# Eight consecutive rows per partition in the expert up weights of a two-block transformer kernel

## The chip, the cores and the metric

The kernel runs on one core of a Trainium2 chip. The metric is the device time of one execution in microseconds. Weights and scratch tensors lie in HBM; the core's 16 DMA engines bring them into SBUF, which has 128 partitions.

## The reference, cut to what matters

Two transformer blocks run in a row on 1024 tokens of width 1024, all in float32, with a context of 256 tokens beside them. The first block has two layers, each ending in a mixture of experts in which each of 16 experts picks its 128 tokens (and, in the first layer, 32 context tokens); the second block has one layer with 32 experts of which each token picks two. What the change touches is the path from a normed row into the experts:

```python
h = rmsnorm(xl, norm2_g) * (1 + sc2) + sh2
aff = jax.nn.softmax((h @ router_w).astype(jnp.float32), axis=-1)
top_aff, idx = lax.top_k(jnp.swapaxes(aff, 1, 2), cap)
xg = jax.vmap(lambda hb, ib: hb[ib])(h, idx)
hid = jax.nn.silu(jnp.einsum('becd,edf->becf', xg, w_gate)) * jnp.einsum('becd,edf->becf', xg, w_up)
y = jnp.einsum('becf,efd->becd', hid, w_down) * top_aff[..., None].astype(h.dtype)
```

`sc2` and `sh2` are the second modulation vectors. They and `norm2_g` have one number for each of the 1024 features. The contraction over the feature `d` (1024) is cut into 8 chunks of 128. Any split of the 1024 features into 8 groups of 128 gives the same sums, as long as the rows `h`, the router's weights, the expert weights and the modulation columns use the same one. The second block is alike, with gate and up weights side by side in one tensor `w_expert_up_2` of 1024 x 1024 per expert.

## The kernel before, in words

The program is a list of stages, each with its own buffers and semaphores and a barrier at its end. Within a stage each engine has its instruction list written out by hand: SP and ACT issue direct DMAs, POOL (GpSimd) issues gathers and scatters with indices, PE multiplies and transposes, DVE (VectorE) and ACT (ScalarE) do the rest. `X` holds the token rows in SBUF, 128 tokens to a tile. `KD` is 8, the number of feature chunks. A tensor read as `(k p)` puts feature `128 k + p` into chunk `k`, partition `p`.

- `Modulating` (from L103) computes the modulation columns of a layer. `load_small` (L132) brings the two gains and four bias vectors as 48 rows of 128 into `small` by six DMAs; `turn_small` (L146) transposes them on PE, `take_small` (L150) copies the result to `smallT`. `products` multiplies with 4 MB of weights per group, `turn` (L174) transposes the two result rows in 8 pieces of 128, `take` copies them, and `finish` (L193) combines them on POOL into `cols`. Groups 0 to 2 are the first modulation, 3 to 5 the second. It runs beside the stages `setup`, `l0out`, `l0route` and `l1route`.
- `route_choice` (L1615), the stages `l0route` and `l1route`: SP loads the router weights `rw` (L1667), then the small vectors and the modulation weights. For each tile ACT writes the normed row `xn` (L1694, three buffers) and issues its store to the scratch tensor `XN`; PE transposes it in 8 pieces (L1749); DVE and ACT apply the columns of half the chunks each. Scores, softmax and the choice of the tokens by DVE follow. A buffer of `xn` is free once its store has landed.
- `choice_experts` (L1918), the stages `l0exp` and `l1exp`: for each expert SP issues the loads of `wg` (L1958), `wu` (L1959) and `wd` (L1962), 2 MB each, two experts deep; `wg` and `wu` wait until the expert two before has been multiplied, `wd` until its down product is done. POOL gathers the 128 (and 32) chosen rows from `XN` (L1970), two experts ahead, and scatters the results into `F` (L1984). PE turns the gathered rows (L2009), DVE applies the columns into `xT` (L2070), PE multiplies with `wg` and `wu` (L2026) and with `wd` (L2043).
- `mix_dispatch` (L3047), the stage `disp`: the same norm, store, transpose and scoring for the second block (L3306, L3347, L3355), and the first loads of the block experts.
- `block_experts` (L3384), the stage `bexp`: blocks of 128 rows, each with the weights of its expert, in a loop over pairs of blocks.

## Time and profile before

| what | value |
|---|---|
| runs of the kernel | 4721.94, 4724.09, 4727.69 us (median 4724.09) |
| span of the profiled execution | 4732.4 us |
| PE busy | 4229.9 us, 89% |
| DVE, ACT, POOL busy | 2033.2, 1069.4, 738.1 us |
| bytes moved by DMA | 769.59 MB, mean 163 GB/s |

The span runs from the first to the last record of one profiled execution; it lies 8.3 us above the median of the unprofiled runs. Busy times are sums of instruction durations. The stages in question lie at 997 to 1094 us (`l0route`), 1095 to 1570 (`l0exp`), 2400 to 2493 (`l1route`), 2493 to 2870 (`l1exp`), the dispatch up to 3982 and `bexp` from there to 4700. In `l0exp` and `l1exp` there are 96 loads of 2 MB, 64 of them of gate and up weights.

### The profile page before, as it was taken

To read this page: it belongs to the slowest core of one execution; us is meant where nothing else is said; L and a number is where in the kernel's file an instruction comes from. 1 tells how busy PE (TensorE), PEld (TensorE's weight loads), DVE (VectorE), ACT (ScalarE), POOL (GpSimd) and SP (SyncE) were. 2 spreads that over 40 slices of the span, in tenths; PEclk is the share of its full clock that TensorE was granted. 3 is DMA by queue.
4 is the path that set the end of the run, shared out by engine and by line. 5 is a ranking of instruction groups with operands and counts; after the bars stand their busy time and mean duration, and the time that the engine had idled before them with its cause. 6 is when DMAs were issued, how large, how long until landed. Compare 5 with 4: busy or idle time off the path is not lost. (4 is left out here: it accounts for less than half of the span.)

```text
span 4732.4 us, 59744 instructions
## 1 busy us (share of the span) xinstructions
PE 4229.9 (89%) x22975; PEld 2790.0 (59%) x22975; DVE 2033.2 (43%) x3879; ACT 1069.4 (23%) x2077; POOL 738.1 (16%) x851
## 2 busy tenths in 40 slices
PE   6998999977999798999968997999788896999996
PEld 4664556445888565566436885776566454444443
DVE  1223556135555322556254452111686666333332
ACT  1112346030000110335130001110564421111111
POOL 0110000301111011000301100000550330222221
PEclk8998999988999899999978998999899897999998
DMA  7115110367887411401169995111532115999997
GB/s 252 36 47 125 23 42 7 129 254 273 274 267 252 138 62 57 108 1 48 44 250 326 338 327 168 49 37 42 144 86 87 59 40 209 316 334 339 334 334 244
DMA packets 366851, 769.59 MB, mean 163 GB/s; under 512 B 59716, under 2 KB 136172, under 8 KB 365384
## 3 DMA queue, kind: packets, MB, share of 16 engines
q1 hardware_dynamic: 337032, 653.92, 40.2%
q0 software_dynamic: 23856, 90.19, 7.4%
q10 hardware_dynamic: 5712, 22.02, 1.2%
q8 instruction: 172, 2.82, 0.2%
q14 instruction: 79, 0.65, 0.0%
HBM read 650.62 MB, written 115.45 MB: 162 GB/s over the span
## 5 line engine op out<-in xcount | busy, mean ns | idle before, releaser
L3537 PE MATMUL bexp_gu<-X,bexp_xT 128*128 128x512 f32 x512 | 227.6, 598 | 3.0 <-DVE bexp_xT L3557 3.0
L3537 PE MATMUL bexp_gu<-bexp_wu,bexp_xT 128*128 128x512 f32 x512 | 225.1, 592 | 3.1 <-DVE bexp_xT L3557 3.1
L625 PE MATMUL p_ring<-p_hT,p_wc 128*128 128x256 f32 x1008 | 220.4, 381 | 4.8 <-DMA p_wc<-in_w_in 4.8
L625 PEld LDWEIGHTS p_ring<-p_hT,p_wc 128*128 128x128 f32 x1008 | 192.3, 191 | 31.6 <-issue 5.2
L3564 DVE TENSOR_SCALAR bexp_ex<-bexp_ex 128x512 f32<-128x512 f32 x32 | 15.1, 471 | 368.7 <-ACT bexp_ex L3492 368.7
L633 PE MATMUL p_ring<-p_wt,p_hT 128*128 128x400 f32 (+2 forms) x480 | 170.8, 516 | 0.0
L3537 PEld LDWEIGHTS bexp_gu<-X,bexp_xT 128*128 128x128 f32 x512 | 97.0, 192 | 119.8 <-issue 116.5
L3537 PEld LDWEIGHTS bexp_gu<-bexp_wu,bexp_xT 128*128 128x128 f32 x512 | 95.9, 190 | 117.7 <-issue 117.7
L1117 PE MATMUL l0mla_scores<-l0mla_kT,l0mla_qT 96*128 96x512 f32 (+1 forms) x312 | 142.9, 546 | 21.1 <-DMA l0mla_qT<-RT 15.3
L2026 PE MATMUL l0exp_gu<-l0exp_xT,l0exp_wg 128*128 128x160 f32 x1024 | 155.0, 305 | 4.5 <-DVE l0exp_xT L2070 4.5
L2026 PE MATMUL l0exp_gu<-l0exp_xT,l0exp_wu 128*128 128x160 f32 x1024 | 151.1, 301 | 1.5 <-DMA l0exp_wu<-in_exp_w_up 1.5
L2026 PEld LDWEIGHTS l0exp_gu<-l0exp_xT,l0exp_wg 128*128 128x128 f32 x1024 | 143.7, 192 | 11.4 <-issue 6.2
L3451 POOL TENSOR_TENSOR bexp_y<-bexp_y,bexp_og 128x1024 f32<-128x1024 f32 x32 | 75.0, 2344 | 481.6 <-ACT bexp_y L3486 481.6
L2043 PE MATMUL l0exp_acc<-l0exp_wd,l0exp_hid 128*32 128x256 f32 (+1 forms) x768 | 144.1, 455 | 2.6 <-DVE l0exp_hid L2085 2.6
L2026 PEld LDWEIGHTS l0exp_gu<-l0exp_xT,l0exp_wu 128*128 128x128 f32 x1024 | 144.0, 192 | 1.9 <-DMA l0exp_wu<-in_exp_w_up 1.9
L1117 PE MATMUL l1mla_scores<-l1mla_kT,l1mla_qT 96*128 96x512 f32 (+1 forms) x288 | 133.8, 551 | 12.3 <-DMA l1mla_qT<-RT 12.3
L3486 ACT ACTIVATE bexp_y<-bexp_acc,slot_gates 128x512 f32<-128x512 f32 x64 | 44.0, 687 | 419.6 <-PE bexp_acc L3525 419.6
L633 PEld LDWEIGHTS p_ring<-p_wt,p_hT 128*128 128x128 f32 x480 | 91.1, 190 | 76.1 <-issue 38.3
L2026 PE MATMUL l1exp_gu<-l1exp_xT,l1exp_wg 128*128 128x128 f32 x1024 | 127.4, 279 | 3.0 <-DMA l1exp_wg<-in_exp_w_gate 3.0
L2026 PEld LDWEIGHTS l1exp_gu<-l1exp_xT,l1exp_wg 128*128 128x128 f32 x1024 | 123.2, 195 | 10.6 <-issue 7.2
L2026 PE MATMUL l1exp_gu<-l1exp_xT,l1exp_wu 128*128 128x128 f32 x1024 | 125.7, 276 | 3.0 <-DMA l1exp_wu<-in_exp_w_up 3.0
L633 PE MATMUL l0proj_ring<-l0proj_wt,l0proj_hT 128*128 128x464 f32 x320 | 126.2, 552 | 0.0
(683 smaller groups left out, 8392.9 us busy)
## 6 DMA issues: line engine op xcount, KB each, us to landing
X<-in_w_expert_up SPq DMA_DIRECT2D x32, 2048.0 KB, 16.0
bexp_wu<-in_w_expert_up SPq DMA_DIRECT2D x32, 2048.0 KB, 16.7
l0exp_wg<-in_exp_w_gate SPq DMA_DIRECT2D x16, 2048.0 KB, 9.3
l0exp_wu<-in_exp_w_up SPq DMA_DIRECT2D x16, 2048.0 KB
l0exp_wd<-in_exp_w_down SPq DMA_DIRECT2D x16, 2048.0 KB, 12.6
l1exp_wg<-in_exp_w_gate SPq DMA_DIRECT2D x16, 2048.0 KB, 9.5
l1exp_wu<-in_exp_w_up SPq DMA_DIRECT2D x16, 2048.0 KB
l1exp_wd<-in_exp_w_down SPq DMA_DIRECT2D x16, 2048.0 KB, 13.1
```

Source lines behind the costliest of these rows:

```text
L625: mm = nc.tensor.matmul(out[:, i * PC:(i + 1) * PC], wc[:, k, b * 128:(b + 1) * 128], hT[ch % 2][:, k, :], start=(k == 0), stop=(k == KD - 1))
L633: mm = nc.tensor.matmul(out[:, at_out:at_out + n], hT[ch % 2][:, k, t * 128:(t + 1) * 128], wt[:, k, s:s + n], start=(k == 0), stop=(k == ...
L1117: mm = nc.tensor.matmul(scores[u % NBUF][:, at:at + n], qT[p % 2][a][:, row:row + 128], k[:, r:r + n], start=True, stop=True)
L2026: mm = nc.tensor.matmul(gu[g % 2][:, h, :], w[j][:, k, f * 128:(f + 1) * 128], xT[j][:, k, :], start=(k == 0), stop=(k == KD - 1))
L2043: mm = nc.tensor.matmul(acc[g % 3][cap * q:cap * (q + 1), 0:n_y], hid[j][:, f, at[s]:at[s] + cap], wd[j][:, f, at_y:at_y + n_y], start=(f ...
L3451: nc.gpsimd.tensor_tensor(y[j][:, :], y[j][:, :], og[:, :], ALU.mult).then_inc(weighed[j], 1)
L3486: nc.scalar.activation(y[j][:, c * 512:(c + 1) * 512], acc[c][:, :], ACT.Copy, scale=gates[:, bass.ds(i * B + j, 1)]).then_inc(y_ready[j], 1)
L3537: mm = nc.tensor.matmul(gu[h][:, :], xT[j][:, k, :], wu[j][h][:, k, :], start=(k == 0), stop=(k == KD - 1))
L3564: nc.vector.tensor_scalar(ex[:, :], ex[:, :], 1.0, None, ALU.add).then_inc(steps[j], 1)
```

## The change

The split of the features changes from `(k p)` to `(p k)`: chunk `k`, partition `p` now holds feature `8 p + k`, so that partition `p` needs the eight consecutive rows `8 p` to `8 p + 7` of a weight matrix. All that meets in the contraction follows: router weights, gate and up weights, the normed rows (ACT reads `X` with a step of eight elements and writes `xn` in the new order, so `XN` holds permuted rows), and the second modulation columns. The three small vectors of the second modulation are no longer transposed but loaded directly into `smallT` with eight numbers per partition; the transposes of the rows in groups 3 and 4 take every eighth element. The down weights and the first modulation stay as they are.

```diff
     def load_small(self, eng):
-        parts = [self.gain1, self.gain2] + [self.b[g * D:(g + 1) * D] for g in (0, 1, 3, 4)]
-        for i, src in enumerate(parts):
+        for i, src in enumerate([self.gain1] + [self.b[g * D:(g + 1) * D] for g in (0, 1)]):
             eng.dma_start(self.small[i * KD:(i + 1) * KD, :], src.rearrange("(k p) -> k p", p=128)).then_inc(self.small_in, 16)
+        for i, src in enumerate([self.gain2] + [self.b[g * D:(g + 1) * D] for g in (3, 4)]):
+            eng.dma_start(self.smallT[:, 3 + i, :], src.rearrange("(p k) -> p k", k=KD)).then_inc(self.small_in, 16)
...
-        self.nc.tensor.transpose(self.turned[:, 0:48], self.small[:, :], self.identity[0:48, 0:48]).then_inc(self.small_turned, 1)
+        self.nc.tensor.transpose(self.turned[:, 0:24], self.small[:, :], self.identity[0:24, 0:24]).then_inc(self.small_turned, 1)
...
         for k in range(KD):
-            tp = self.nc.tensor.transpose(self.turned[:, 64 + 2 * k:66 + 2 * k], self.rows[n % 2][:, k * 128:(k + 1) * 128], self.identity[0:2, 0:2])
+            chunk = slice(k * 128, (k + 1) * 128) if self.groups[n] < 3 else slice(k, D, KD)
+            tp = self.nc.tensor.transpose(self.turned[:, 64 + 2 * k:66 + 2 * k], self.rows[n % 2][:, chunk], self.identity[0:2, 0:2])
...
-                sp.dma_start(rw[:, :, 0:E], router_w.rearrange("(k p) e -> p k e", p=128)).then_inc(w_in, 16)
+                sp.dma_start(rw[:, :, 0:E], router_w.rearrange("(p k) e -> p k e", k=KD)).then_inc(w_in, 16)
...
-                    nc.scalar.activation(xn[n % 3][:, :], X[:, t, :], ACT.Copy, scale=ssum[:, t:t + 1]).then_inc(normed, 1)
+                    nc.scalar.activation(xn[n % 3][:, :].rearrange("p (k a) -> p k a", k=KD), X[:, t, :].rearrange("p (a k) -> p k a", k=KD), ACT.Copy,
+                                         scale=ssum[:, t:t + 1]).then_inc(normed, 1)
...
-                    sp.dma_start(wg[j][:, :, :], w_gate[e].rearrange("(k p) n -> p k n", p=128)).then_inc(gate_in[j], 16)
-                    sp.dma_start(wu[j][:, :, :], w_up[e].rearrange("(k p) n -> p k n", p=128)).then_inc(up_in[j], 16)
+                    sp.dma_start(wg[j][:, :, :], w_gate[e].rearrange("(p k) n -> p k n", k=KD)).then_inc(gate_in[j], 16)
+                    sp.dma_start(wu[j][:, :, :], w_up[e].rearrange("(p k) n -> p k n", k=KD)).then_inc(up_in[j], 16)
...
-                            sp.dma_start(wu[j][h][:, :, :], w_up[bass.ds(e, 1), :, h * FF:(h + 1) * FF].rearrange("e (k p) n -> p (e k) n", p=128)).then_inc(landed[j], 16)
+                            sp.dma_start(wu[j][h][:, :, :], w_up[bass.ds(e, 1), :, h * FF:(h + 1) * FF].rearrange("e (p k) n -> p (e k) n", k=KD)).then_inc(landed[j], 16)
```

The same edits stand in `mix_dispatch` for its router weights, its norm and its first loads, and in `block_experts` for the loads ahead of the loop. In `take_small` and `finish` only the columns' numbers follow.

## Rows read from the trace of the kernel before

**Rows 1.** The page: each engine's busy time, share of the span, instructions
```profile
PE 4229.9 (89%) x22975; PEld 2790.0 (59%) x22975; DVE 2033.2 (43%) x3879; ACT 1069.4 (23%) x2077; POOL 738.1 (16%) x851
```

**Rows 2.** Windows: stretch, length, busy PE PEld DVE ACT POOL, clock, DMA share, GB/s
```profile
1095.00:1104.00 9.00, 0.00 (x0) 0.00 (x0) 0.00 (x0) 0.00 (x0) 5.05 (x6) 0.50 0.86 278
1200.00:1540.00 340.00, 340.00 (x2315) 274.95 (x2314) 191.28 (x460) 14.61 (x48) 56.63 (x46) 1.00 0.80 264
2512.00:2522.00 10.00, 7.48 (x52) 7.48 (x53) 1.75 (x4) 0.47 (x2) 0.00 (x0) 0.82 1.03 398
2560.00:2860.00 300.00, 299.42 (x2078) 248.29 (x2076) 148.37 (x348) 15.27 (x55) 33.77 (x26) 1.00 0.91 312
4100.00:4600.00 500.00, 500.00 (x1372) 236.14 (x1371) 180.33 (x276) 56.59 (x92) 118.99 (x112) 1.00 0.98 334
```

**Rows 3.** Waits of PE in the two choice-expert stages: total, times, longest
```profile
PE l0exp_turned L2009 <- DMA l0exp_xg<-XN,ctx_idx: 13.0, 1, 13.0
PE l0exp_gu L2026 <- DMA l0exp_wu<-in_exp_w_up: 1.5, 1, 1.5
PE l1exp_turned L2009 <- DMA l1exp_xg<-XN,lat_idx: 10.8, 1, 10.8
PE l1exp_gu L2026 <- DMA l1exp_wg<-in_exp_w_gate: 3.0, 1, 3.0
PE l1exp_gu L2026 <- DMA l1exp_wu<-in_exp_w_up: 3.0, 1, 3.0
```

**Rows 4.** Timeline, first layer's experts: start, duration, engine, instruction, idle before it
```profile
1095.87 1.17 POOL L1970 DMA_INDIRECT l0exp_xg<-XN,lat_idx  x1 [5.50 <-POOLq L87]
1106.37 1.97 PE L2009 MATMUL l0exp_turned<-identity,l0exp_xg 128*128 128x128 f32 x8 [12.97 <-DMA l0exp_xg<-XN,ctx_idx]
```

**Rows 5.** DMA queues, 1103 to 1110 us: packets, MB, share of 16 engines
```profile
q0 software_dynamic: 367, 1.26, 64.7%
q1 hardware_dynamic: 367, 0.72, 39.0%
```

**Rows 6.** Tile l0route_xn: durations ns; its engine's idle time; who waited for it
```profile
L1694 ACT ACTIVATE l0route_xn<-X,energy x10: 1132/1148/1176, 998.8 to 1027.1; 128x1024 f32<-128x1024 f32 x10
  DMA XN<-l0route_xn: 5.7, 4
  PE l0route_turned L1749: 12.9, 5
```

**Rows 7.** Small ACT and DVE operations by line: ns min/median/max
```profile
L2811 ACT ACTIVATE gs_decay<-gs_b x2: 201/202/203, 3760.7 to 3760.8; 128x10 f32<-128x10 f32 x2
L287 ACT ACTIVATE setup_e<-setup_v x1: 229/229/229, 4.0 to 4.0; 128x32 f32<-128x32 f32 x1
L301 DVE TENSOR_TENSOR silu<-setup_v,setup_e x2: 168/172/175, 4.9 to 5.0; 128x16 f32<-128x16 f32 x2
L3186 DVE TENSOR_TENSOR disp_upto<-disp_upto,disp_both x8: 191/192/193, 3951.2 to 3952.8; 128x32 f32<-128x32 f32 x8
```

**Rows 8.** Timeline of SP's and POOL's issues, one expert of the second layer
```profile
2595.92 0.37 SPq L1958 DMA_DIRECT2D l1exp_wg<-in_exp_w_gate  x1
2606.37 0.37 SPq L1962 DMA_DIRECT2D l1exp_wd<-in_exp_w_down  x1
2607.90 1.57 POOL L1984 DMA_INDIRECT F<-l1exp_y,lat_idx  x1 [19.17 <-DVE l1exp_y L2099]
2609.77 0.98 POOL L1970 DMA_INDIRECT l1exp_xg<-XN,lat_idx  x1 [0.30 <-issue]
2617.96 0.37 SPq L1958 DMA_DIRECT2D l1exp_wg<-in_exp_w_gate  x1
```

**Rows 9.** Timeline of the dispatch stage, ACT, one tile of eight
```profile
3905.99 1.06 ACT L3297 ACTIVATE disp_gated<-X 128x1024 f32<-128x1024 f32 x1 [3.48 <-DVE X L3125]
```

**Rows 10.** By line: issue of the router load; weight loads of the row transposes
```profile
L1667 SPq DMA_DIRECT2D l0route_rw<-in_router_w x1: 384/384/384, 997.4 to 997.4; - x1
L181 PEld LDWEIGHTS l0route_modturned<-identity,l0route_modrow x32: 134/158/224, 1050.5 to 1079.8; 2*128 2x128 f32 x32
```

More of the change, by code:

```diff
@@ L111, in __init__ @@
         self.bias_row = st.sb(f"{tag}bias_row", [2, 2, D])
-        self.small = st.sb(f"{tag}small", [48, 128])
+        self.small = st.sb(f"{tag}small", [24, 128])
         self.smallT = st.sb(f"{tag}smallT", [128, 6, KD])
@@ L207, in finish @@
         col = self.col[c % 2][:, :, :]
-        shift = across(2 + 2 * half + scale)
+        shift = across(3 * half + 1 + scale)
         if scale == 0:
@@ L216, in finish @@
         po.wait_ge(self.col_stepped, START + before + 2)
-        self.nc.gpsimd.tensor_tensor(self.cols[:, 2 * half, :, :], col, across(half), ALU.mult).then_inc(self.col_made, 1)
+        self.nc.gpsimd.tensor_tensor(self.cols[:, 2 * half, :, :], col, across(3 * half), ALU.mult).then_inc(self.col_made, 1)
     def store(self, eng, n):
@@ L3305, in scale @@
                         act.wait_ge(row_turned, START + n - NX + 1)
-                    nc.scalar.activation(xn[n % NX][:, :], X[:, CTX_TILES + n, :], ACT.Copy, scale=energy[:, n:n + 1]).then_inc(normed, 1)
+                    nc.scalar.activation(xn[n % NX][:, :].rearrange("p (k a) -> p k a", k=KD), X[:, CTX_TILES + n, :].rearrange("p (a k) -> p k a", k=KD), ACT.Copy,
+                                         scale=energy[:, n:n + 1]).then_inc(normed, 1)
                 act.wait_ge(eps_made, START + 1)
```

10 lines of the change are left out of this document (5 added, 5 removed).

## The prediction

> **What bounds the kernel now.** I read the page first. TensorE (PE) is busy for 89% of the span [rows 1], so a faster load is worth something only where PE stands still for it. The loads that change sit in three expert stages, and the table by windows says what holds each of them in its steady part. In the first layer's experts PE is busy 340.00 of 340 us while the DMA engines are at 0.80 of their time; in the second layer's experts it is 299.42 of 300 us at a DMA share of 0.91; in the block experts of the second block it is 500 of 500 us at 0.98 [rows 2]. The reader is to see two things there: PE is the bound in all three, and the DMA engines, though nearly full, never make it wait. The list of waits, cut to those stages, agrees. PE waits for a weight or for gathered rows only where a stage starts: 13.0 and 1.5 us in the first layer, 10.8, 3.0 and 3.0 us in the second [rows 3]. The whole prize of faster weight loads lies in these starts, and the longest waits are not for weights. They are for the gather of the chosen rows.
>
> **Part one: the row size of the loads.** For `wg` and `wu` of the choice experts (64 loads of 2 MB) the new order makes the eight rows of a partition one run of 16 KB, where there were eight runs of 2 KB. For the block experts nothing of the kind happens: half of each 4 KB row is taken, so the runs stay 2 KB, 1024 to a load, only in another order. Bytes are equal everywhere. In the steady part I cost this at nothing, because PE covers it [rows 2].
>
> The start of a stage is different, since weights and gather go through the same engines at once. The gather is issued at 1095.87 and PE begins on its rows at 1106.37 [rows 4]. The view of the DMA queues over seven microseconds of that start shows how the two queues share: 367 packets of the software queue (gather, 1.26 MB) and 367 of the hardware queue (weights, 0.72 MB) [rows 5]. Equal counts at unequal bytes mean that an engine takes one packet from the one and one from the other. A pair costs 7 us x 16 engines / 367 = 0.305 us, and the weight packet's part of it is 0.39 x 7 x 16 / 367 = 0.119 us.
>
> If a 16 KB run is one packet in this turn-taking, each 4 KB gather row waits for 16 KB of weights. One engine moves at best 398 GB/s / 16 = 24.9 bytes per ns in the fullest window of a start [rows 2], so 16 KB take 0.66 us, which is 0.54 us more than the 0.119 of today. First layer: 128 + 32 gathered rows over 16 engines are 10 turns, 5.4 us later. Second layer: 128 rows are 8 turns, 4.3 us later. Weights are there to oppose all of them: the two loads in front of the gather hold 4.2 MB, 16 packets of 16 KB to an engine. In the first nine microseconds of the stage the engines moved 278 GB/s x 9 us = 2.5 MB [rows 2], some of it already gathered rows; I estimate that 1.3 to 2 MB of weights are gone when the gather starts, which leaves 8 to 11 packets to an engine, about as many as there are turns.
>
> Something comes back. With the gather later, `wg` and `wu` have landed before PE asks for them. In the first layer the 1.5 us wait for `wu` goes: 5.4 - 1.5 = +3.9 us. In the second the 3.0 us wait for `wu` goes; of the other 3.0 us, for `wg`, PE spends nearly all while DVE still modulates the gathered rows (8 of them, one after the other, between the transposes and the first product), so I let only 0.3 us come back. 4.3 - 3.0 - 0.3 = +1.0 us. What is late next in both is the gather itself. Sum of part one: **+4.9 us**. Its bounds are -7.5 us (no delay of the gather, all three weight waits gone whole: 1.5 + 3.0 + 3.0) and +9.7 us (5.4 + 4.3, nothing comes back).
>
> Does the same turn-taking hurt in the steady part? The timeline of one expert says no. Gate and up weights are issued at 2595.92, the down weights at 2606.37, the scatter of the results at 2607.90, the next gather at 2609.77, and the next gate weights only at 2617.96 [rows 8]. At 398 GB/s the 4.2 MB of gate and up need 10.5 us and are through when the scatter starts. Scatter and gather share the engines with the down weights, whose 4 KB rows are unchanged. Cost 0; if that cover were gone, the gather would be some 5 us later and still has more than a cycle of 22 us until its turn.
>
> **Part two: strided reads on ScalarE (ACT).** Each normed row tile is now read from `X` at a step of 32 bytes and written in order: 10 + 8 + 8 instructions. One takes 1.148 us today [rows 6]. No row shows an ACT read of this size at such a step, so I bound it: below 0 is excluded, as the elements are the same in number; above I take a doubling. The nearest rows are small but speak clearly. An ACT exponential of 10 elements at a step of 512 bytes took 202 ns, one of 32 elements in order 229 ns [rows 7]: 1.2 ns for each further element, the normal pace, with nothing left over for the step. On VectorE a product of 16 elements, whose inner pairs are 32 bytes apart so that every element lies elsewhere than the last, took 172 ns, and one of 32 in order 192 ns [rows 7]: again the same line. I take **0**, by these rows.
>
> The Trainium skill speaks against this part: "SBUF — State Buffer", section "Door 1: The DMA port swizzle", says that SBUF has 16-byte lines, that at least two hits on a line are needed for full bandwidth, and that each access crossing to a new line pays. Eight floats apart no two accesses share a line, so by that page all 26 instructions would be slower. The rows named just above show no such charge at 10 and 16 elements; the measured case of 1024 does not exist in this trace, so the rule stays as a rival.
>
> **Part three: the second modulation columns.** Three of six small loads of 4 KB now go straight into place with 32-byte pieces over 128 partitions, and the transpose and its copy shrink from 48 to 24 columns. The number of issues on SP's queue stays. The issue of a load over 128 partitions took 0.384 us [rows 10], so three of them can push the modulation weights behind them by at most 1.2 us in a stage and more likely by 0.3; at every place PE is busy with other things or waits for a 4 MB load afterwards. The transposes of the modulation rows now take every eighth element; there are 48 of that kind in the three stages, with a weight load of 0.158 us each [rows 10]. Doubled, that is 7.6 us at most, spread over a chain that runs beside VectorE's selection of the rows. I take 0 for both and keep +3 us as the upper end.
>
> **Part four: router weights.** The same 64-byte pieces as before, in another order. One answer: 0.
>
> **The sum.** 0 + 4.9 + 0 + 0 = +4.9 us on the profiled execution, 4732.4 + 4.9 = 4737.3 us of span. That execution's span lies 8.3 us above the median of the runs (4724.09), so on the median I forecast **4729.0 us**, +0.10%. A measurement of this kernel can tell about 0.2% (9.4 us) from no change; this is below it.
>
> **Rivals.**
> A. *Large runs don't delay the gather* (they are cut up, or turns go by bytes). For it: no row shows 16 KB runs against another queue. Then only the weight waits go, counted as above: -1.5 - 3.3 = -4.8, **4719.3 us**. Chance 0.25.
> B. *The strided reads cost* (the other side). Decides from about 0.5 us an instruction upward. In the routing stages PE waits for ACT's normed rows, 12.9 us in the first layer [rows 6], so ACT is on the path there. Doubled: first layer 10 x 1.15 = 11.5, less the 5.7 us in which ACT today waits for the store of the row before [rows 6], 5.8 us; second layer, eight tiles in the same pattern, eight tenths of it, 4.6 us; in the dispatch stage ACT idles 3.48 us per tile [rows 9] and hides all but the last two, 2.3 us. Together 12.7 on top of 4.9: **4741.7 us**, +0.37%. Against it: rows 7.  Chance 0.12.
> C. *The new order reads memory more slowly.* The second layer's experts have 9% of a 22.04 us cycle to give, 2.0 us; the 10.5 us of gate and up use that up once they run 16% slower. At 25% slower each expert is 1.5 us longer, 14 x 1.5 = 21 us: **4750 us**. Nothing in the profile speaks for it. Chance 0.06.
> D. *A gain of more than 9.4 us.* It would have to come from somewhere other than the weight waits, which sum to less. Chance 0.07.
> The forecast keeps 0.50.
>
> **How the numbers follow.** Same: forecast and A, 0.75. Slower by over 0.2%: B and C, 0.18. Faster by over 0.2%: D, 0.07. The range reaches from the lower bound of part one (4724.1 - 7.5) to B: 4717 to 4742, which leaves out C and D.
>
> **What would show it.** In the changed trace: packets of 16 KB in the two choice-expert stages and unchanged 2 KB ones in the block experts; the first transposes of the first layer's experts 5 us later after the gather's issue than the 10.5 us of today [rows 4], of the second layer's 4 us; no wait for `wu` at either start; steady PE windows still full [rows 2]; normed-row instructions at 1.15 us. If these stand at 2.3 us, B holds; if the gather lands as before, A. The prediction is wrong if PE waits for weights inside a steady stage, or if its own pace per expert changes.

## Result and the profile after

Eleven runs of each, on the same chip: the kernel before 4725.79 us (median), the changed kernel 4735.15 us. The ratio is 1.0021, 95% interval 1.0012 to 1.0030: slower by 9.4 us, between 5.7 and 14.2. The forecast was 4729.0. The profiled execution of the changed kernel has a span of 4734.7 us against 4732.4; single stages that the change doesn't touch differ by up to 5 us between the traces of this study (the stage of tiles `da`: 252.6 to 257.4), so the two spans are not set against each other below. Stage lengths are.

The page of the changed kernel, busy time by engine (against [rows 1]):

```profile
PE 4225.1 (89%) x22975; PEld 2786.6 (59%) x22975; DVE 2034.4 (43%) x3879; ACT 1094.3 (23%) x2077; POOL 737.8 (16%) x851
```

TensorE is as busy as before. ScalarE (ACT) has 24.9 us more, with the same number of instructions. The rows of the norm show where (against [rows 6]): one takes 2.147 us instead of 1.148, TensorE waits 16.0 us for them instead of 12.9, and ScalarE waits 1.7 us for the store of a row instead of 5.7.

```profile
L1696 ACT ACTIVATE l0route_xn<-X,energy x10: 2131/2147/2214, 998.5 to 1030.1; 128x1024 f32<-128x1024 f32 x10
  DMA XN<-l0route_xn: 1.7, 2
  PE l0route_turned L1752: 16.0, 6
```

So the strided read is not free. The windows of the changed kernel (stretch, length, busy PE, PEld, DVE, ACT, POOL, granted clock, DMA share, GB/s; against [rows 2]):

```profile
1200.00:1540.00 340.00, 340.00 (x2328) 276.15 (x2327) 191.01 (x460) 14.92 (x49) 56.66 (x46) 1.00 0.77 267
2560.00:2860.00 300.00, 300.00 (x2078) 248.45 (x2077) 148.73 (x348) 15.00 (x54) 33.80 (x26) 1.00 0.90 311
4100.00:4600.00 500.00, 500.00 (x1372) 235.93 (x1371) 180.37 (x276) 55.97 (x92) 119.26 (x113) 1.00 0.98 336
```

The steady parts are as full as before: 16 KB runs cost and give nothing there. At the starts of the two choice-expert stages the waits of TensorE have changed (against [rows 3]):

```profile
PE l0exp_turned L2012 <- DMA l0exp_xg<-XN,ctx_idx: 17.2, 1, 17.2
PE l0exp_gu L2029 <- DVE l0exp_xT L2073: 4.5, 1, 4.5
PE l1exp_turned L2012 <- DMA l1exp_xg<-XN,lat_idx: 14.1, 1, 14.1
PE l1exp_gu L2029 <- DVE l1exp_xT L2073: 2.7, 1, 2.7
```

The gather is 4.2 and 3.3 us later, and no wait for a weight is left. The view of the DMA queues over the same seven microseconds as [rows 5] shows why:

```profile
q1 hardware_dynamic: 161, 2.38, 82.0%
q0 software_dynamic: 159, 0.59, 20.5%
```

Equal counts again, but a packet of the weights is now 14.8 KB on average: 145 of the 161 are of 16 KB, the others of 4 bytes. A pair takes 7 x 16 / 160 = 0.70 us where it took 0.305. In the block experts the weight packets are of 2 KB as before.

A table that the experiments will fill: the time from TensorE's last instruction of one stage to its last of the next, from the timelines, in us, for the six stages that the change touches. The last two columns are the sum against that of the kernel before, and the difference of the medians of the timed runs, each kernel against the runs of the kernel before that were timed beside it. One of the twelve runs of e7 took 5779.9 us at a granted clock of 0.731 and is left out.

| kernel | route 1 | experts 1 | route 2 | experts 2 | dispatch | block experts | sum | medians |
|---|---|---|---|---|---|---|---|---|
| before | 101.0 | 476.7 | 96.4 | 376.8 | 103.4 | 719.1 | 0 | 0 |
| changed | 103.6 | 476.3 | 99.2 | 377.3 | 106.2 | 719.2 | +8.4 | +9.4 |
| stride in the transposes (e1) | 101.4 | 483.5 | 96.6 | 377.1 | 105.5 | 719.4 | +10.1 | +11.3 |
| first weights in pieces (e2) | 102.2 | 477.6 | 99.4 | 377.0 | 107.0 | 719.1 | +8.9 | +11.0 |
| gather first (e3) | 101.8 | 481.5 | 96.5 | 377.1 | 105.4 | 719.4 | +8.3 | +12.6 |
| latent rows in order (e5) | 102.4 | 475.4 | 96.6 | 376.9 | 105.9 | 719.5 | +3.3 | +4.3 |
| the same again (e11) | 101.1 | 476.0 | 96.9 | 375.3 | 105.5 | 719.5 | +0.8 | +2.9 |
| that with 2 KB runs (e9) | 101.8 | 473.9 | 95.9 | 376.7 | 105.7 | 719.5 | +0.1 | +0.5 |
| before with strided norm (e6) | 102.5 | 474.7 | 96.5 | 375.6 | 105.5 | 719.1 | +0.3 | +2.7 |
| before with shared norm (e7) | 98.0 | 476.2 | 95.8 | 376.4 | 105.7 | 719.2 | -2.3 | -3.5 |
| shared norm and e5 (e8) | 99.6 | 475.1 | 96.3 | 377.2 | 105.5 | 719.5 | -0.3 | +3.5 |
| early stream (e10) | 106.9 | 473.8 | 97.3 | 375.6 | 105.5 | 719.1 | +4.9 | +7.2 |
| late wait (e12) | 102.3 | 474.2 | 93.1 | 377.3 | 103.2 | 719.1 | -4.2 | +1.0 |

Three columns warn the reader. The dispatch stage has the same code in the kernels before, e7, e10 and e12, and took 103.4, 105.7, 105.5 and 103.2 us in them. Its 2.8 us between the first two rows is therefore no evidence. The two stages of experts have the same code in the kernels before, e6, e7, e10 and e12, and took 473.8 to 476.7 and 375.6 to 377.3 us. Part of that can be seen in single rows. These are the last down product of the first layer's experts, before and after:

```profile
1559.35 10.70 PE L2043 MATMUL l0exp_acc<-l0exp_wd,l0exp_hid 128*128 128x512 f32 x48 [2.57 <-DVE l0exp_hid L2085]
```

```profile
1562.93 9.00 PE L2046 MATMUL l0exp_acc<-l0exp_wd,l0exp_hid 128*128 128x512 f32 x48 [2.57 <-DVE l0exp_hid L2088]
```

After the same wait of 2.57 us the granted clock fell to 0.50 for a part of this product in the kernel before, and not in the changed one; that is 1.7 us. In the second layer it is the other way round, and e5 and e11, which are the same kernel, differ in it there.

In the first routing stage the kernels with the same code differ by up to 1.4 us (103.6 and 102.2 in the changed one and e2; 102.4 and 101.1 in e5 and e11), so its +2.6 us is evidence for some 1 to 3 us. The +2.8 us of the second routing stage stands firm: 99.2 and 99.4 in the changed kernel and e2, 96.4 to 96.9 in the kernels before, e1, e3, e5, e6 and e11.

### The profile page after: what moved, and what is told of

Read it like the earlier page. It is cut to its first block and busy times, and to the rows that moved or that the text cites. A ratio compares the mean times of both kernels' runs of the same rounds, so it can differ in the third digit from the quotient of the medians.

```text
span 4734.7 us, 59744 instructions
## 1 busy us (share of the span) xinstructions
PE 4225.1 (89%) x22975; PEld 2786.6 (59%) x22975; DVE 2034.4 (43%) x3879; ACT 1094.3 (23%) x2077; POOL 737.8 (16%) x851
## 5 line engine op out<-in xcount | busy, mean ns | idle before, releaser
L3455 POOL TENSOR_TENSOR bexp_y<-bexp_y,bexp_og 128x1024 f32<-128x1024 f32 x32 | 75.1, 2346 | 481.5 <-ACT bexp_y L3490 481.5
L1119 PE MATMUL l1mla_scores<-l1mla_kT,l1mla_qT 96*128 96x512 f32 (+1 forms) x288 | 133.6, 550 | 12.4 <-DMA l1mla_qT<-RT 12.4
## 6 DMA issues: line engine op xcount, KB each, us to landing
l0exp_wd<-in_exp_w_down SPq DMA_DIRECT2D x16, 2048.0 KB, 12.4
l1exp_wu<-in_exp_w_up SPq DMA_DIRECT2D x16, 2048.0 KB, 12.6
```

The lines of the kernel that those rows point to most:

```text
L1119: mm = nc.tensor.matmul(scores[u % NBUF][:, at:at + n], qT[p % 2][a][:, row:row + 128], k[:, r:r + n], start=True, stop=True)
L3455: nc.gpsimd.tensor_tensor(y[j][:, :], y[j][:, :], og[:, :], ALU.mult).then_inc(weighed[j], 1)
```

## The experiments

The theory after the first look (S): the strided reads are dear and lie on the path of the routing stages. Its rival (G): what was forecast, the gather's delay costs 4.9 us and the strides nothing.

**e1: the stride on TensorE instead of ScalarE.** The norm copies in order; each transpose takes every eighth element, here, in the stages of experts, in the dispatch stage and in the block experts.

```diff
-nc.scalar.activation(xn[n % 3][:, :].rearrange("p (k a) -> p k a", k=KD), X[:, t, :].rearrange("p (a k) -> p k a", k=KD), ACT.Copy,
-                     scale=ssum[:, t:t + 1]).then_inc(normed, 1)
+nc.scalar.activation(xn[n % 3][:, :], X[:, t, :], ACT.Copy, scale=ssum[:, t:t + 1]).then_inc(normed, 1)
...
-tp = nc.tensor.transpose(turnedP[n % 2][:, k, :], xn[n % 3][:, k * 128:(k + 1) * 128], identity[:, :])
+tp = nc.tensor.transpose(turnedP[n % 2][:, k, :], xn[n % 3][:, k:D:KD], identity[:, :])
```

> The changed kernel with the permutation moved from ScalarE to TensorE: the norm reads and writes its row in order again (all three stages), and each transpose takes every eighth element of the row instead of 128 consecutive ones. The 16 KB runs and the permuted columns stay. Theory S (the strided read of 1024 elements costs ScalarE about 1.0 us each and that lies on the path at the start of the two routing stages and of the dispatch stage: 2.55 + 2.8 + 2.8 = 8.2 us between the two traces): this kernel is 8 us faster than the changed one, within 1.5 us of the kernel before, the norm back at 1.15 us. Theory G (what was forecast: the delayed gather costs 4.9 us and the strided reads nothing): no gain over the changed kernel, still 5 to 10 us behind the kernel before. Rival P (TensorE pays for a stride as ScalarE does): the 8 transposes of 128x128 in the steady part of an expert take more than 1.04 us; at twice that, 32 gathers and some 30 blocks and 26 row tiles lose about 1 us each, and the kernel is 60 to 80 us slower.

Measured: 4735.78 us, ratio to before 1.0024 (1.0013 to 1.0034). By the time alone theory S would have fallen. The stages tell more: the routing stages are 2.2 and 2.6 us shorter than in the changed kernel (101.4 and 96.6), and the first layer's experts lost 7 us. There rival P holds, but only for the small transposes of the context rows. First the rows of the changed kernel, then of e1 (weight load and product; ns min/median/max):

```profile
L2015 PEld LDWEIGHTS l0exp_turnedC<-identity,l0exp_xg x128: 132/138/219, 1114.8 to 1524.9; 32*128 32x128 f32 x128
L2015 PE MATMUL l0exp_turnedC<-identity,l0exp_xg x128: 220/222/311, 1114.8 to 1524.9; 32*128 32x32 f32 x128
```

```profile
L2014 PEld LDWEIGHTS l0exp_turnedC<-identity,l0exp_xg x128: 181/201/203, 1112.8 to 1528.9; 32*128 32x128 f32 x128
L2014 PE MATMUL l0exp_turnedC<-identity,l0exp_xg x128: 269/269/312, 1112.8 to 1528.9; 32*128 32x32 f32 x128
L2011 PEld LDWEIGHTS l0exp_turned<-identity,l0exp_xg x128: 186/191/231, 1110.9 to 1527.8; 128*128 128x128 f32 x128
L2011 PE MATMUL l0exp_turned<-identity,l0exp_xg x128: 272/274/479, 1110.9 to 1527.9; 128*128 128x128 f32 x128
```

A strided weight load costs some 50 to 60 ns more in both shapes. Behind a product of 272 ns it is hidden; behind one of 222 ns it is not, and 16 x 8 of these cost 0.047 us each, 6 us in all. About the rest of the 7 us is the last down product of the stage, which has its slow part here as in the kernel before.

**e2: the first weights in pieces.** The run size is undone for the first two experts of a stage alone.

```diff
-sp.dma_start(wg[j][:, :, :], w_gate[e].rearrange("(p k) n -> p k n", k=KD)).then_inc(gate_in[j], 16)
-sp.dma_start(wu[j][:, :, :], w_up[e].rearrange("(p k) n -> p k n", k=KD)).then_inc(up_in[j], 16)
+for w, src, landed in ((wg, w_gate, gate_in), (wu, w_up, up_in)):
+    rows = src[e].rearrange("(p k) n -> p k n", k=KD)
+    for k in range(KD if e < B else 1):
+        part = slice(k, k + 1) if e < B else slice(0, KD)
+        sp.dma_start(w[j][:, part, :], rows[:, part, :]).then_inc(landed[j], 16)
...
```

> The changed kernel with one thing undone: the gate and up weights of the first two experts of each choice stage are loaded as eight transfers of one row per partition (2 KB runs), all later ones as 16 KB runs. Theory T (an engine takes one packet of each queue in turn, a 16 KB run is one packet, so each gathered 4 KB row waits for 16 KB of weights): from the issue of the gather to TensorE's first transpose 10.5 us in the first layer and 8.5 in the second as in the kernel before, instead of 14.8 and 11.8; the waits for weights come back (1.5 us; 3.0 and 3.0), and the time of the whole changes by less than 2 us. Rival Q (the gather is late for another reason, such as the order of rows in memory): it stays at 14 to 15 and 11 to 12 us.

Measured: 4735.45 us, ratio 1.0021 (1.0012 to 1.0031), and these waits:

```profile
PE l0exp_turned L2015 <- DMA l0exp_xg<-XN,ctx_idx: 12.3, 1, 12.3
PE l0exp_gu L2032 <- DMA l0exp_wu<-in_exp_w_up: 2.8, 1, 2.8
PE l1exp_turned L2015 <- DMA l1exp_xg<-XN,lat_idx: 9.9, 1, 9.9
PE l1exp_gu L2032 <- DMA l1exp_wg<-in_exp_w_gate: 3.0, 1, 3.0
PE l1exp_gu L2032 <- DMA l1exp_wu<-in_exp_w_up: 2.8, 1, 2.8
```

With short runs in the same order of rows the gather is on time again, so rival Q falls: it is the long runs that delay it, as theory T has it. From its issue to the first transpose it takes 9.8 and 7.7 us, 0.7 and 0.8 less than in the kernel before; here eight transfers bring what one brought there, so the two are not quite alike. And the whole gains nothing: with the gather on time the weights are late again, 2.8 us in the first layer where it was 1.5.

**e3: no weights beside the first gather.** On top of e1, SyncE holds the first weights back until the first rows are there.

```diff
+if e == 0:
+    sp.wait_ge(gathered[0], 16 * NS)
 sp.dma_start(wg[j][:, :, :], w_gate[e].rearrange("(p k) n -> p k n", k=KD)).then_inc(gate_in[j], 16)
```

> As the kernel with the stride in the transposes, and SyncE waits for the first gathered rows before it issues the first weights of a choice stage. Without weights beside them the rows (0.65 MB and 0.52 MB, some 1.6 and 1.3 us at the fullest rate, plus the latency of a transfer) should be there 5 to 6 us after the gather's issue instead of 10.5 and 8.5 in the kernel before. Then transposes and modulation take 7.4 us until the first weights are wanted, and the first 2 MB land 7 to 8 us after their issue. Theory (the gather bounds the start, weights fit behind it): 3 to 4 us gained at each of the two starts, 6 to 8 us against the kernel before. Rival: the second 2 MB (up weights) are then wanted before they have landed, a wait of 3 to 5 us takes the gain back, and the kernel is within 2 us of the kernel before.

Measured: 4737.08 us, ratio 1.0029 (1.0018 to 1.0040). The theory's gain of 6 to 8 us against the kernel before did not come. Its base, e1, already stands 11.3 us behind the kernel before, and against e1 this kernel is 1.3 us slower. The rows came early, and the rival took it all back:

```profile
PE l0exp_gu L2030 <- DMA l0exp_wg<-in_exp_w_gate: 8.1, 1, 8.1
PE l0exp_turned L2013 <- DMA l0exp_xg<-XN,ctx_idx: 7.9, 1, 7.9
PE l0exp_gu L2030 <- DMA l0exp_wu<-in_exp_w_up: 2.1, 1, 2.1
```

From the end of the routing stage to the first product of the down weights it is 50.3 us here, 50.6 in e1, 50.2 in e2, 50.7 in the changed kernel and 49.3 in the kernel before. TensorE's waits alone don't explain that. Up to that product they are 18.1 us here and 21.2 in e1, so 3 us of wait were saved and 0.3 arrived. The products before it ran longer at the slow clock: the granted clock is 0.50 from 1112 to 1123.5 us here, where TensorE is busy for 9.36 us, and also 0.50 from 1111 to 1123 in e1, where it is busy for 7.52. The account of the first part, further down, comes back to this.

**e4: probes of single costs.** Nothing of the reference is computed.

> Nothing of the reference is computed: probes of single costs alone. One: ScalarE and VectorE copy 1024 fp32 elements per partition with a step of 1, 2, 3, 4, 6 and 8 elements in the read, of 2, 4 and 8 in the write, in the changed kernel's form (k a from a k), and 16, 64 and 256 elements at steps 1 and 8. Theory L (a read fetches lines of 16 bytes and an element that has its line alone pays for it): ScalarE 1.15 us at steps 1 and 2, 2.1 at 4 and beyond; a small count shows little of it (16 elements: 0.02 us). Rival M (every step but 1 pays): 2.1 at step 2 as well. Two: TensorE transposes 128 columns and multiplies 512 columns with steps 1, 2, 4, 8 in the operand. Three: two loads of 2 MB each with runs of 2, 4, 8 and 16 KB while a software-queue load of 128 rows of 4 KB runs beside them, three times each, and that load alone. Theory T (packets in turn, a run is one packet): the row load takes longer with the run, about 8 turns of (run / 24.9 bytes per ns): 0.7, 1.3, 2.6 and 5.3 us above its time alone. Rival: runs above some size are cut into packets of equal size, and the time stops growing there.

ScalarE, 1024 elements, by the step of the read (the name of the output tile), then the changed kernel's form (`perm`), a step of eight in the write, and 16 and 256 elements. Columns: busy us, mean ns of one, idle before.

```profile
L3848 ACT ACTIVATE m_r_one<-X,m_scale 128x1024 f32<-128x1024 f32 x6 | 6.9, 1147 | 14.9 <-DMA X<-in_x 14.7
L3852 ACT ACTIVATE m_r_two<-X,m_scale 128x1024 f32<-128x1024 f32 x6 | 7.3, 1211 | 0.2
L3856 ACT ACTIVATE m_r_three<-X,m_scale 128x1024 f32<-128x1024 f32 x6 | 9.9, 1649 | 0.2
L3860 ACT ACTIVATE m_r_four<-X,m_scale 128x1024 f32<-128x1024 f32 x6 | 12.6, 2106 | 0.2
L3868 ACT ACTIVATE m_r_eight<-X,m_scale 128x1024 f32<-128x1024 f32 x6 | 12.8, 2131 | 0.2
L3872 ACT ACTIVATE m_perm<-X,m_scale 128x1024 f32<-128x1024 f32 x6 | 12.8, 2132 | 0.2
L3884 ACT ACTIVATE m_wide<-X,m_scale 128x1024 f32<-128x1024 f32 x6 | 12.7, 2124 | 0.2
L3892 ACT ACTIVATE m_nxvi_one<-X,m_scale 128x16 f32<-128x16 f32 x6 | 1.8, 308 | 0.2
L3896 ACT ACTIVATE m_nxvi_eight<-X,m_scale 128x16 f32<-128x16 f32 x6 | 1.9, 321 | 0.2
L3908 ACT ACTIVATE m_ncclvi_one<-X,m_scale 128x256 f32<-128x256 f32 x6 | 3.0, 507 | 0.2
L3912 ACT ACTIVATE m_ncclvi_eight<-X,m_scale 128x256 f32<-128x256 f32 x6 | 4.5, 752 | 0.2
```

Steps of 1 and 2 are nearly alike, 3 lies between, from 4 on (16 bytes and more) an element costs 0.91 to 0.96 ns more (the lowest, 2079 ns for one, is at a step of 6). Theory L holds and rival M falls. At 16 elements the charge is 13 ns, at 256 it is 245. VectorE pays less, and TensorE pays where the strided operand is the moving one (step 1 first, then 8):

```profile
L3921 DVE TENSOR_SCALAR m_r_one<-X,m_scale 128x1024 f32<-128x1024 f32 x6 | 4.5, 752 | 156.5 <-ACT m_ncclvi_eight L3912 156.3
L3941 DVE TENSOR_SCALAR m_r_eight<-X,m_scale 128x1024 f32<-128x1024 f32 x6 | 6.8, 1142 | 0.2
L4003 PE MATMUL m_acc<-X,identity 128*128 128x512 f32 x64 | 27.6, 592 | 0.0
L4009 PE MATMUL m_acc<-X,identity 128*128 128x512 f32 x64 | 58.9, 1097 | 0.0
```

The third part of the probe: 128 rows of 4 KB by the software queue, beside two loads of 2 MB whose runs are 2, 4, 8 and 16 KB, and alone (last number: us from issue to landing).

```profile
d_row_one<-in_x POOLq DMA_DIRECT2D x3, 512.0 KB, 7.7
d_row_two<-in_x POOLq DMA_DIRECT2D x3, 512.0 KB, 7.8
d_row_four<-in_x POOLq DMA_DIRECT2D x3, 512.0 KB, 8.5
d_row_eight<-in_x POOLq DMA_DIRECT2D x3, 512.0 KB, 10.9
d_row_alone<-in_x POOLq DMA_DIRECT2D x3, 512.0 KB, 3.5
```

The wait grows with the run and does not stop at a size, as theory T has it, but its sizes are wrong. The expectation gave 0.7, 1.3, 2.6 and 5.3 us above the time alone; measured are 4.2, 4.3, 5.0 and 7.4. Most of that is there with the shortest runs already: beside the weights the first packet of the rows starts some 4 us after the issue, and alone 1.2 us after it. From 2 to 16 KB it is 3.2 us where the expectation would give 4.6 (5.3 less 0.7). Turns of one to one are seen here with long runs alone: while 128 rows pass, 140 to 146 packets of 16 KB runs pass beside them, but 318 to 357 of 2 KB runs. The step from 2 to 4 KB costs 0.1, so runs of 4 KB would have been free here.

**e5 and e11: the runs without the strides.** Latent rows stay in order and their transposes take every eighth element; the two context tiles are permuted by the norm, so that the small transposes read in order. e11 is the same kernel once more.

```diff
+if NB > 2 and tile_at[n][2] == 2:
     nc.scalar.activation(xn[n % 3][:, :].rearrange("p (k a) -> p k a", k=KD), X[:, t, :].rearrange("p (a k) -> p k a", k=KD), ACT.Copy,
                          scale=ssum[:, t:t + 1]).then_inc(normed, 1)
+else:
+    nc.scalar.activation(xn[n % 3][:, :], X[:, t, :], ACT.Copy, scale=ssum[:, t:t + 1]).then_inc(normed, 1)
...
```

> The runs of 16 KB without the stride on ScalarE and without the stride where it was dear: latent rows stay in order and their 128x128 transposes take every eighth element (1.05 against 1.04 us for eight); the two context tiles are permuted by the norm as in the changed kernel, so that the 32-row transposes of the context rows go back from 1.06 to 0.68 us. Theory S: the routing stages keep what the kernel with the stride in the transposes won there (2.2 and 2.6 us), the first layer's experts lose their 16 x 0.38 = 6 us again, and the kernel is 5 to 8 us faster than the changed one, within 2 us of the kernel before. What is left between it and the kernel before is the effect of the runs alone (with the small loads): by the traces +1.3 us in the first layer and -1.2 in the second, about nothing; by the forecast +4.9. Rival G (the forecast's first part is right for the whole time): 4.9 us slower than before.

> The kernel with latent rows in order and context rows permuted once more, beside its pair with runs of 2 KB. Theory N: within 1.5 us of that pair; theory R: 3 to 5 us slower than it. Against the kernel before, by its first measurement, 4.0 us slower; if that was chance, by the sum of its stages 1 to 2 us.

Measured: 4730.97 us and 4730.30 us, ratio 1.0008 both times (0.9999 to 1.0017). The 6 us of the small transposes are back, as are the 2.6 and 2.3 us of the second routing stage. What is left against the kernel before is 3 to 4 us, twice, each time with an interval (0 to 8 us) that just reaches 1.

**e6: the stride alone.** The kernel before, with both sides of the norm in steps of eight, so that the order of the row is unchanged.

```diff
-nc.scalar.activation(xn[n % 3][:, :], X[:, t, :], ACT.Copy, scale=ssum[:, t:t + 1]).then_inc(normed, 1)
+every = lambda a: a.rearrange("p (a k) -> p k a", k=KD)
+nc.scalar.activation(every(xn[n % 3][:, :]), every(X[:, t, :]), ACT.Copy, scale=ssum[:, t:t + 1]).then_inc(normed, 1)
```

> The kernel before with one thing added: ScalarE reads and writes the rows of the norm in steps of eight elements on both sides, so that the row comes out in its old order and nothing else changes. Theory S: each norm takes 2.13 us instead of 1.15 and the stages lose as in the changed kernel, 2.5, 2.8 and 1 to 2.8 us, so 6 to 8 us slower than before (ratio 1.0013 to 1.0017). Theory G: within 1 us of before. If a strided write costs on top of a strided read, the norm takes 3.1 us and the loss is above 12 us.

Measured: 4729.38 us, ratio 1.0008 (0.9999 to 1.0016). The norm takes what it takes in the changed kernel, and a write in steps adds nothing to a read in steps:

```profile
L1695 ACT ACTIVATE l1route_xn<-X,energy x8: 2125/2138/2189, 2400.3 to 2425.5; 128x1024 f32<-128x1024 f32 x8
```

But the price in time is 2.7 us by the medians, where theory S gave 6 to 8. The interval, -0.5 to 7.6 us, excludes neither that nor nothing. The stages say more: the second routing stage is not longer at all, and theory S had 2.8 us there. The first is 1.5 us longer, which is about what kernels with the same code differ by.

**e9: the run size alone.** e5, with gate and up weights of all experts in two transfers each, even and odd rows of a partition.

```diff
+for odd in range(2):
-    sp.dma_start(wg[j][:, :, :], w_gate[e].rearrange("(p k) n -> p k n", k=KD)).then_inc(gate_in[j], 16)
+    sp.dma_start(wg[j][:, odd::2, :], w_gate[e].rearrange("(p k) n -> p k n", k=KD)[:, odd::2, :]).then_inc(gate_in[j], 16)
...
```

> The kernel with latent rows in order and context rows permuted (16 KB runs, no stride on the path of ScalarE but for the two context tiles), with the run size alone undone: gate and up weights of all experts come in two transfers each, even and odd rows of a partition, so that every run is 2 KB again and no two join. Theory R (the runs of 16 KB cost something that the stage lengths hide): it is 3 to 5 us faster than its pair with 16 KB runs, which stood 4.0 us behind the kernel before (interval 0 to 8). Theory N (the run size is worth nothing over the whole kernel; what is left is the context tiles and the small loads): within 1.5 us of its pair. In both the gather's wait goes back to 10 to 11 and 8 to 9 us and waits for weights return.

Measured: 4727.88 us, ratio 1.0003 (0.9994 to 1.0012), 2.4 us under e11 in the same comparison. That lies between the two theories and within the intervals of both; the runs cost between nothing and some 5 us. The gather's waits are back at 12.4 and 10.6 us (16.7 and 14.0 in e11).

**e7 and e8: the norm shared by two engines.** An attempt to beat both kernels. Norms of even tiles of the routing stages go to VectorE (0.752 us by the probe), those of odd tiles stay on ScalarE; e7 from the kernel before, e8 from e5.

```diff
+nc.vector.tensor_scalar(into, row, ssum[:, t:t + 1], None, ALU.mult).then_inc(normed_v, 1)
...
```

> The kernel before with the norms of even tiles in the two routing stages on VectorE (0.75 us by the probe) and those of odd tiles on ScalarE, everything in the old order. If ScalarE's norm bounds the start of these stages (TensorE waits 12.9 and 15.1 us for it, of which 5 to 7 us after the first tile), then 2 to 4 us are gained in each, 4 to 8 us in all. Rival: VectorE has its own half of the modulation behind each tile (four instructions) and becomes the late one; then nothing is gained, or up to 3 us lost.

> Both: the rows of the first of these four kernels and the shared norm of the third. If the effects are independent and the runs of 16 KB are worth nothing, it equals the third within 2 us; if the runs cost 4.9 us, it is that much slower than the third.

Measured: e7 4723.14 us, ratio 0.9995 (0.9987 to 1.0004); e8 4730.21, ratio 1.0005 (0.9996 to 1.0014). The first routing stage is 3.1 us shorter in e7, the second 0.7. e8 is 7.1 us over e7 by the medians and 4.9 by the means: a third comparison in which the rows of e5 stand behind the old ones.

**e10 and e12: the modulation weights first.** The second routing stage barely moved in e6 and e7, so something else ends it. These rows say what (line, operation, busy, idle before it): the first is the kernel before, the second the changed one.

```profile
L1900 DVE TENSOR_TENSOR l1route_ahead<-l1route_chosen,l1route_other 16x128 f32<-16x128 f32 x1 | 2.0, 1983 | 6.7 <-ACT l1route_other_f L1736 6.7
```

```profile
L1903 DVE TENSOR_TENSOR l1route_ahead<-l1route_chosen,l1route_other 16x128 f32<-16x128 f32 x1 | 2.0, 1985 | 9.3 <-ACT l1route_other_f L1739 9.3
```

VectorE has chosen its rows and waits for a small copy on ScalarE. That copy is queued behind the evictions of the modulation, and these wait for six loads of 4 MB. e10 (from e7) issues the first of these loads ahead of the router's weights and the small loads, and lets VectorE make the copies. The transposes of the small vectors move from behind the second row tile to behind the sixth.

```diff
 sp.sem_inc(opened, 1)
+mod.load(sp, 0)
 sp.wait_ge(blanked, START + 1)
...
-nc.scalar.activation(other[:, :], chosen[32:32 + E, ::-1], ACT.Copy).then_inc(moved, 1)
+V_.tensor_copy(other[:, :], chosen[32:32 + E, ::-1]).then_inc(moved, 1)
```

> The kernel before with the shared norm, and two more edits in the routing stages: the first 4 MB of modulation weights are issued before the router's weights and the small loads, and the copies of the chosen values that VectorE waited for at the end of the selection (6.7 to 9.3 us, behind ScalarE's evictions, which wait for that stream) are made by VectorE itself. Theory M (the end of the second routing stage is set by the stream of modulation weights, which starts 8.1 us after the stage before it ends, and by ScalarE's order behind it): the stream starts 3.5 to 4 us earlier, each routing stage is 2 to 5 us shorter than in the kernel with the shared norm alone, 4 to 9 us in all, 6 to 12 us under the kernel before. Rival: the gates' rows, the last product of the modulation and its store end the stage anyway, and only the earlier start counts: 2 to 4 us. Against it: the router's weights and small loads then land behind 4 MB, at 16 us, and TensorE may wait for them.

Measured: 4734.60 us, ratio 1.0017 (1.0008 to 1.0026), slower. TensorE waits for the router's weights before its first transpose, and they now stand behind 4 MB; in the timeline that transpose begins with this wait (last bracket):

```profile
1009.28 3.67 PE L1754 MATMUL l0route_turned<-identity,l0route_xn 128*128 128x128 f32 x16 [19.65 <-DMA l0route_rw<-in_router_w]
```

e12, from e10, moves that wait to where the weights are used (another wait, for `blanked`, moves with it).

```diff
-pe.wait_ge(w_in, START + 16)
 for n in range(6):
     turn(n)
...
+pe.wait_ge(w_in, START + 16)
 score(0)
```

> The kernel with the early stream, with its fault mended: TensorE waits for the router's weights (which now land behind 4 MB of modulation weights) only before the first scores, no longer before the first transpose. In the kernel with the early stream that wait was 19.65 us against 7.30 us for the first norm in the kernel with the shared norm, and the first product of the modulation came at 45.6 us of the second routing stage instead of 36.4, so that its buffer came free late. Theory M: the first transposes are back at 7.3 us, the stream runs ahead from 4.6 us on, VectorE's selection no longer waits 7.5 us for ScalarE, and the second routing stage is 2 to 6 us shorter than with the shared norm alone (95.8), the first up to 3 (98.0); the whole 5 to 10 us under the kernel before. Rival: the last product of the modulation and the gates' rows end the stages as before, and it stays within 3 us of the kernel with the shared norm alone (2 us under the kernel before).

Measured: 4726.71 us, ratio 0.9999 (0.9990 to 1.0008). The second routing stage is 93.1 us, 2.7 shorter than in e7, as theory M has it; which of its two edits did it was not tried apart. The first is 4.4 us longer than in e7, and in it norms wait longer for the stores of the rows before (the tile `xn`'s engines sat idle 20.1 us for `XN` there, 12.1 in e7); that the early stream delays these stores was not shown by itself. The whole is 1.0 us over the kernel before and not 5 to 10 under it. No kernel of this study beats the kernel before by more than its measurement is uncertain.

## Why the prediction was right or wrong

The time lies in the range, 6 us above the forecast. The outcome held likeliest, no more than 0.2% of difference, was missed by a hair (0.21%, with an interval of 0.12 to 0.30% that lies on both sides). The steps fared differently.

- *What bounds the kernel.* Right: steady windows full, nothing lost or won there, the block experts unchanged in every kernel of the table.
- *Part one, the mechanism.* Right for this kernel: one packet from each queue in turn. Counts are equal again, 161 and 159, and the rival A (no delay) fell with these rows, with e2 and e9, where 2 KB runs took the delay away, and with the probe. **The size of the term**: a pair takes 0.70 us, not 0.85, which is 0.395 more than before; ten turns make 4.0 and eight 3.2 us, and 4.2 and 3.3 were seen where 5.4 and 4.3 were forecast. The weight packet's part of a pair is 0.82 x 112 / 161 = 0.57 us, not 0.66, and the gathered row's is 0.14 where it was 0.20.
- *Part one, what comes back.* The waits for weights did as forecast: 1.5 in the first layer, 3.0 and 0.3 in the second. **The sum has no term for the clock.** TensorE's granted clock is 0.50 (1.2 GHz) when a stage of experts starts and 1.00 (2.4 GHz) later, and how many products fall before its rise decides as much as the waits do. These are the first product groups of the second layer's experts behind the very first one, before and after, and the first of them in e6, which has the weights and runs of the kernel before:

```profile
2514.52 2.89 PE L2026 MATMUL l1exp_gu<-l1exp_xT,l1exp_wu 128*128 128x128 f32 x16 [2.98 <-DMA l1exp_wu<-in_exp_w_up]
2517.20 2.78 PE L2026 MATMUL l1exp_gu<-l1exp_xT,l1exp_wg 128*128 128x128 f32 x16
2519.82 1.95 PE L2026 MATMUL l1exp_gu<-l1exp_xT,l1exp_wu 128*128 128x128 f32 x16
```

```profile
2516.60 2.63 PE L2029 MATMUL l1exp_gu<-l1exp_xT,l1exp_wu 128*128 128x128 f32 x16
2519.07 1.95 PE L2029 MATMUL l1exp_gu<-l1exp_xT,l1exp_wg 128*128 128x128 f32 x16
```

```profile
2512.10 2.05 PE L2027 MATMUL l1exp_gu<-l1exp_xT,l1exp_wu 128*128 128x128 f32 x16 [2.36 <-DMA l1exp_wu<-in_exp_w_up]
```

The very first group of sixteen takes 3.75, 3.79 and 3.78 us in the three, and a group at a granted 1.00 takes 1.95. In the kernel before the clock rose while TensorE waited (0.93 from 2512 to 2516 us) and fell again (0.51 from 2516 to 2519), and the two groups behind the wait lost another 1.8 us by it. That fall is not the price of the wait: in e6 TensorE waited 2.36 us at the same place, and the group behind it took 2.05. The kernels e9 and e12 are like e6, and e7 and e10 like the kernel before.

So the first two kernels alone mislead. Between them the first layer's start, from the end of the routing stage to the first product of the down weights, is 1.35 us longer and the second's 1.2 us shorter, +0.2 in all. Eleven kernels load the gate and up weights with one run size from the first expert to the last and don't hold them back. Their first layer's starts, in us, all counted from the end of the routing stage: TensorE's idle time up to the first down product (the wait for the gather included), the rise of the granted clock to 1.00 for good, and that product:

| kernel | runs | TensorE's waits | clock at 1.00 after | whole start |
|---|---|---|---|---|
| before | 2 KB | 18.9 | 29.5 | 49.3 |
| e7 | 2 KB | 17.8 | 29.7 | 48.9 |
| e6 | 2 KB | 18.5 | 24.6 | 47.3 |
| e12 | 2 KB | 18.0 | 24.6 | 46.9 |
| e10 | 2 KB | 18.0 | 23.5 | 46.4 |
| e9 | 2 KB | 18.1 | 23.0 | 46.4 |
| changed | 16 KB | 21.7 | 29.8 | 50.7 |
| e1 | 16 KB | 21.2 | 29.2 | 50.6 |
| e11 | 16 KB | 21.2 | 29.1 | 50.1 |
| e5 | 16 KB | 21.2 | 28.0 | 49.6 |
| e8 | 16 KB | 21.2 | 27.5 | 49.3 |

The waits are longer by 3.1 us on average (forecast: 3.9), and the whole start by 2.5 (47.5 and 50.0). Within a form the start follows the rise of the clock and hardly the waits, and the kernel before has the longest start of its form. In the second layer the waits are longer by 0.3 us (forecast: 1.0), and the start is 40.2 us on average with 2 KB runs and 39.8 with 16 KB runs. Over the whole stages (changed, e5, e8 and e11 against the six) it is +0.8 and +0.3 us, with a scatter of up to 3 us. Part one is thus worth some 1 to 2 us in the stages, and e9 against e11 gives 2.4 in time; that is less than half of the forecast's 4.9 and, by the scatter and by the interval of e9, not safely more than nothing.
- *Part two.* **This step failed.** It took 0 from rows with 10 and 16 elements [rows 7]. By the probe the charge there is 13 ns for 16 elements on ScalarE and nothing on VectorE: unlike instructions can't be told apart at that size, and the rows bore no conclusion. At 1024 elements the charge is 1.0 us. The rule of the Trainium skill that was set aside ("SBUF — State Buffer", "Door 1: The DMA port swizzle": 16-byte lines, at least two hits on each) is what the probe shows for ScalarE: 1.147 and 1.211 us at steps of 4 and 8 bytes, 1.649 at 12 bytes, 2.106 at 16 and 2.131 at 32. VectorE, by the same probe, pays 0.39 us and not a doubling.
- *Rival B, its price.* The mechanism was true, but its price of 12.7 us was too high; alone (e6) it cost 2.7 us by the medians, and 7.6 at the upper end of the interval. In the first routing stage the wait for stores gave back 4.0 of ten microseconds, as worked out, but at most 1.5 of the other 6.0 reached the end of the stage in e6. In the second none did, since something else ends it. In the dispatch stage it can't be told from the stage's own scatter. Where the rest of the first stage's 6.0 us is hidden was not settled.
- *Part three.* **The cover that it named was not there.** It said that TensorE is busy or waits for a 4 MB load anyway, and that the chain of the modulation runs beside the selection. In the second routing stage this chain is what ends the stage: VectorE had already waited 6.7 us for it before the change. With the small loads the first modulation load is issued 0.7 us later (8.1 to 8.8 us after the end of the stage before), and with strides and loads together the third product of the modulation starts at 54.2 instead of 52.2 us. The last load lands at 84.6 instead of 83.1 us, in the changed kernel and in e2, and at 83.1 to 83.6 in e1, e3, e5, e6, e9 and e11. That stage then takes 99.2 and 99.4 us in the two kernels that have both, and 95.9 to 96.9 in those with one or the other. So most of its 2.8 us belongs to neither part alone; how the two add up (stores of the rows beside the stream, I suppose) was not shown.
- *Part four.* Nothing points to a cost; it was not tried alone.
- *The sum.* By the medians the strides alone cost 2.7 us and the rest 4.3, 2.9 and 7.1 in three comparisons; together they cost 9.4. That the rest comes out near the forecast's 4.9 is in part luck: of that, the run size is some 1 to 2.4 us, and what else the rest holds can't be placed in a stage. This stays open, and so does whether the parts add up: each interval is 8 to 10 us wide.

## What to carry to other kernels

Read the cost of a stride from an instruction of the same size, or measure it: a charge per element can't be seen in rows of ten elements, and 32 bytes between floats nearly double a long ScalarE copy. A larger run is not simply better: it makes every packet of another queue wait longer, and where both are needed before work can begin, holding one back gained nothing here (e3). One trace of each kernel is not enough to price a start: with the same run size and waits within 1.1 us of each other it took 46.4 to 49.3 us, by when the clock rose. Before a chain is called covered, look at who waits for its last instruction; in the second routing stage a small copy, queued behind a slow chain on the same engine, held up VectorE's last steps for 6.7 us.

## What the runs showed of the hardware

- ScalarE: 1.12 and 1.18 ns per element at steps of one and two floats, 2.03 to 2.08 from four on, reading or writing, and no more when both are strided. VectorE: 0.73 at a step of one and 1.12 at eight.
- TensorE: a strided weight load takes about 190 ns instead of 140; it costs nothing behind a product of 272 ns and 47 ns behind one of 222. A strided moving operand of 512 columns takes 1.10 us instead of 0.59.
- Two queues took packets in equal numbers at the start of the first layer's experts, with 2 KB runs (367 and 367) and with 16 KB runs (161 and 159). In the probe that is so beside 16 KB runs (140 to 146 packets to 128 rows) and not beside 2 KB runs (318 to 357). 128 rows of 4 KB land after 3.5 us alone, 7.7 beside 2 KB runs, 10.9 beside 16 KB runs.
- Sixteen products of 128x128 weights with 128 columns take 3.8 us at a granted clock of 0.50 and 1.95 at 1.00. A wait doesn't settle by itself whether the clock falls: at the start of the second layer's experts it fell behind a wait of 2.98 us in the kernel before and not behind one of 2.36 us in e6, and at the end of the first layer's it fell behind a wait of 2.57 us in the kernel before and not in the changed one (48 products of 512 columns in 10.70 and 9.00 us).
